# A depthwise convolution's taps on TensorE: five tiles as bands of 32 channels x 4 phases, laid out in DRAM, and a key norm one piece later

## The chip, the cores and the metric
One core of one Trainium2 chip runs the whole program. The metric is the device time of one execution, in microseconds (us); below it stands beside the span, the time from the first to the last instruction of one profiled execution.

## What is computed
A small decoder trunk on a sequence of 512 rows of 1024 channels in float32: a Conformer convolution layer, then a layer of differential attention, each followed by a gated feed-forward block. What the change touches is the first layer and one norm of the attention layer:

```python
def causal_depthwise_conv(u, w, b):           # w: 31 x 1024, one filter of 31 taps per channel
    y = lax.conv_general_dilated(u, w.reshape(width, 1, c), window_strides=(1,),
        padding=[(width - 1, 0)], dimension_numbers=('NWC', 'WIO', 'NWC'), feature_group_count=c)
    return y + b

def conformer_conv_module(x, ...):
    h = rms_norm(x, norm_g)
    u = h @ pw1_w + pw1_b
    u = u[..., :D_MODEL] * jax.nn.sigmoid(u[..., D_MODEL:])
    u = causal_depthwise_conv(u, dw_w, dw_b)
    u = jax.nn.silu(layer_norm(u, ln_g, ln_b))
    return x + u @ pw2_w + pw2_b
...
hk = rms_norm(x, kv_norm_g)                   # its mean square per row is what the "key norm" sums
k_sh = rms_norm((hk @ w_k).reshape(b, s, N_HEADS, 2, HEAD_DIM), k_norm_g)
```

## The kernel before, in words
The activations lie transposed: channels on the 128 partitions, eight tiles of 128 channels, 512 columns of sequence. Every weight matrix comes from one `stream` in units of 1 MB on SP's DMA queue into a ring of two raw slots (`w_raw`); ScalarE makes the high part of each (`split_weights`, L553), VectorE the low part (L828), and TensorE makes three float32r products for each pair (L1231). A projection unit is 48 such products.

**The convolution.** The first projection (pw1) has eight units. For each, VectorE scales the two halves (L926, L930), ScalarE takes the sigmoid (L610) and VectorE multiplies into `conv_u` (L940). Tiles 0 to 3 get their taps on VectorE: ScalarE makes the first (L623), `convolve` the other 30 (L912, L919) and the addition of two chains (L903), in pieces laid between other work. Tiles 4 to 7 get them on TensorE. ScalarE regroups each into `u2` (L619): 64 channels x 2 phases (even and odd columns) on the 128 partitions, 271 columns. A band is a matrix in which a channel's taps lie on the diagonals; TensorE makes 16 matmuls of 128x128 weights against 256 columns for it (L1304), two bands a tile, eight in all, three PSUM banks in turn (`CONV`). ScalarE copies the two phases back to `conv_c` (L630). The bands are built in DRAM by SP: `fill` writes zeros (L413), `scatter` writes single taps along the diagonals (L426), `load_band` reads rows of 2048 elements, which overlap, to 64 partitions at a time (L418), twice a band. The first two bands go into `w_raw`, the others into `band_sb`.

**The mean of the layer norm** over channels is a sum of eight matmuls with ones (L1295), laid between the bands; the last of tiles 3, 6 and 7 come after the last band. Then VectorE takes the mean away (L964, L967), and the variance follows (L1325).

**The order.** Each engine works through its own list in program order. SP's list is written out by hand: weights of units 2 and 3, the four fills, units 4 and 5, two scattered tiles, units 6 and 7, two scattered tiles, four bands, and then bands as they come free, with the first two units of pw2 among them (L451). Loads of unit n wait until unit n-2 is split.

**The key stage.** Its products are made in pieces of 12 matmuls (`dense`, L1388). After the first two, TensorE sums the squares of the residual by four small matmuls (L1397), which need GpSimd's last addition (L508); ScalarE and VectorE take the root two pieces later.

## Time and profile before

| | before |
|---|---|
| median of 3 runs | 1226.53 us (1226.29 to 1227.96) |
| the profiled execution | 1225.06 us |
| its span | 1223.3 us |
| mean granted TensorE clock | 0.993 of full |
| busy: TensorE / VectorE / ScalarE / GpSimd | 1199.7 / 788.6 / 504.6 / 61.4 us |
| DMA: packets, data | 34614, 116.77 MB |

Times of instructions are from the start of the span. "PE" is TensorE's matmul, "PEld" its weight load, which can overlap the matmul before; DVE is VectorE, ACT ScalarE, POOL GpSimd, SPq the queue on which SP issues DMAs. Matmuls are pipelined: a record's duration is longer than the distance to the next, so paces are read from starts or from totals. A float32 matmul shows as two records, a float32r one as one.

### The profile page before, as it was taken

The numbers are of one execution on the slowest core, as the hardware profiler recorded it, in microseconds if no ns is written. First come the engines' busy times: TensorE is split into PE (matmuls) and PEld (weight loads), VectorE is DVE, ScalarE is ACT, GpSimd is POOL, SyncE is SP. The second block draws the span as 40 slices with busy tenths as digits, with TensorE's granted clock in tenths as the row PEclk, the third lists the DMA queues.
The fourth block names the chain that finished last, engine by engine and source line by source line (L and its number), as shares of the span: only waits on it lengthen the run. The fifth ranks groups of instructions, "written<-read, shape, count | busy, mean of one in ns | idle before, by whom it ended". The sixth has DMA issues, their size and how long they took to land.

```text
span 1223.3 us, 16391 instructions
## 1 busy us (share of the span) xinstructions
PE 1199.7 (98%) x6106; PEld 1008.7 (82%) x6106; DVE 788.6 (64%) x1083; ACT 504.6 (41%) x814; POOL 61.4 (5%) x76
## 2 busy tenths in 40 slices
PE   8999969999999999999999999999999999999998
PEld 7888838888888888887899999987788888888887
DVE  6997945577536663676467676775677447753664
ACT  6332154543214431344656656544544224321441
POOL 1000001100000000001212021100000000000000
PEclk9999989999999999999999999999999999999999
DMA  8564802233322333223321221130232323332222
GB/s 302 137 129 113 217 19 66 73 104 103 103 72 100 103 103 103 73 82 98 103 90 39 70 70 52 56 101 7 97 102 77 131 69 103 103 103 73 99 77 95
DMA packets 34614, 116.77 MB, mean 95 GB/s; under 512 B 18304, under 2 KB 18432, under 8 KB 21888
## 3 DMA queue, kind: packets, MB, share of 16 engines
q1 hardware_dynamic: 34560, 116.03, 30.4%
q8 instruction: 36, 0.59, 0.2%
q14 instruction: 18, 0.15, 0.0%
HBM read 109.60 MB, written 6.49 MB: 95 GB/s over the span
## 4 chain that ended last, share of the span: by engine, by line
PE 92%; DVE 4%; ACT 3%; issue 1%; DMA 0%; POOL 0%; SPq 0%; POOLq 0%; DVEq 0%; ACTq 0%
PE bank L1231 71%; PE bank L1388 9%; PE bank L1304 5%; PE bank L1453 2%; PE bank L1422 1%; PE bank L1325 1%; DVE w_lo L836 1%; PE bank L1295 1%; PE bank L1270 1%; PE bank L1407 1%; ACT prob L790 0%; ACT xg_hi L570 0%; ACT w_hi L563 0%; DMA w_raw<-stream 0%; PE bank L1426 0%
## 5 line engine op out<-in xcount | busy, mean ns | idle before, releaser
L1231 PE MATMUL bank<-xg_hi,w_hi 128*128 128x512 f32 x832 | 326.7, 393 | 1.6 <-DVE xg_lo L844 1.6
L1231 PE MATMUL bank<-xg_lo,w_hi 128*128 128x512 f32 x832 | 323.8, 389 | 0.0
L1231 PE MATMUL bank<-xg_hi,w_lo 128*128 128x512 f32 x832 | 323.7, 389 | 0.0
L553 ACT ACTIVATE w_hi<-w_raw 128x2048 fp32r<-128x2048 f32 x79 | 150.7, 1907 | 149.8 <-PE bank L1231 147.1
L828 DVE TENSOR_TENSOR w_lo<-w_raw,w_hi 128x2048 fp32r<-128x2048 f32 x79 | 182.8, 2314 | 30.9 <-ACT w_hi L553 30.9
L1231 PEld LDWEIGHTS bank<-xg_hi,w_hi 128*128 128x128 f32 x832 | 156.2, 188 | 36.3 <-issue 2.2
L1231 PE MATMUL bank<-act_hi,w_hi 128*128 128x512 f32 x448 | 177.3, 396 | 7.5 <-DVE act_lo L981 7.2
L1231 PEld LDWEIGHTS bank<-xg_lo,w_hi 128*128 128x128 f32 x832 | 156.2, 188 | 33.8 <-issue 1.7
L1231 PEld LDWEIGHTS bank<-xg_hi,w_lo 128*128 128x128 f32 x832 | 156.2, 188 | 32.5
L705 ACT ACTIVATE ffn_t<-ffn_u,par 128x512 f32<-128x512 f32 x88 | 72.0, 818 | 268.7 <-DVE ffn_u L1051 268.7
L1231 PE MATMUL bank<-act_lo,w_hi 128*128 128x512 f32 x448 | 175.3, 391 | 0.0
L1231 PE MATMUL bank<-act_hi,w_lo 128*128 128x512 f32 x448 | 175.1, 391 | 0.0
L1388 PE MATMUL bank<-w_hi,xg_hi 128*128 128x256 f32 x384 | 113.5, 296 | 0.0
L1388 PE MATMUL bank<-w_hi,xg_lo 128*128 128x256 f32 x384 | 109.2, 284 | 0.0
L1388 PE MATMUL bank<-w_lo,xg_hi 128*128 128x256 f32 x384 | 109.1, 284 | 0.0
L1231 PEld LDWEIGHTS bank<-act_hi,w_hi 128*128 128x128 f32 x448 | 84.6, 189 | 27.8 <-issue 8.3
L1058 DVE SCALAR_TENSOR_TENSOR ffn_t<-ffn_u,par,ffn_t 128x512 f32<-128x512 f32 x88 | 65.9, 749 | 56.1 <-ACT ffn_t L705 56.1
L1231 PEld LDWEIGHTS bank<-act_hi,w_lo 128*128 128x128 f32 x448 | 84.7, 189 | 17.9
L1231 PEld LDWEIGHTS bank<-act_lo,w_hi 128*128 128x128 f32 x448 | 84.7, 189 | 17.3 <-issue 0.2
L996 DVE TENSOR_TENSOR x<-bank,x 128x512 f32<-128x512 f32 x48 | 33.0, 689 | 91.9 <-PE bank L1231 91.9
L1051 DVE TENSOR_TENSOR ffn_u<-bank,rs 128x512 f32<-128x512 f32 x88 | 60.6, 688 | 42.4 <-PE bank L1231 42.3
L1388 PEld LDWEIGHTS bank<-w_hi,xg_hi 128*128 128x128 f32 x384 | 74.1, 193 | 0.2 <-DVE w_lo L836 0.2
(160 smaller groups left out, 1448.8 us busy)
## 6 DMA issues: line engine op xcount, KB each, us to landing
w_raw<-stream SPq DMA_DIRECT2D x87, 1024.0 KB, 4.9
band_sb<-band SPq DMA_DIRECT2D x12, 512.0 KB, 6.9
w_raw<-stream SPq DMA_DIRECT2D x8, 768.0 KB, 4.3
band<-band_sb SPq DMA_DIRECT2D x4, 1056.0 KB, 12.3
x<-x_t SPq DMA_DIRECT2D x8, 256.0 KB, 5.8
w_raw<-band SPq DMA_DIRECT2D x4, 512.0 KB, 6.7
out_t<-x SPq DMA_DIRECT2D x8, 256.0 KB, 2.0
w_raw<-stream SPq DMA_DIRECT2D x2, 512.0 KB, 4.7
```

The costliest lines, as they stand in the source:

```text
L553: act.activation(w_hi[:, j, :], w_raw[:, j, :], ACT.Copy).then_inc(w_hi_done, 1)
L705: act.activation(ffn_t[:, 2 * j + s, :], ffn_u[:, 2 * j + s, FTAPS - 1:UP], ACT.Identity, bias=p("ffn_dw_b", at + t), scale=p("ffn_dw_w", ...
L828: dve.tensor_tensor(w_lo[:, j, :], w_raw[:, j, :], w_hi[:, j, :].bitcast(F32), sub).then_inc(w_lo_done, 1)
L836: got = dve.scalar_tensor_tensor(out=w_lo[:, j, cols], in0=w_raw[:, j, cols], scalar=p(row_gain[n], k), in1=w_hi[:, j, cols].bitcast(F32), ...
L996: new = dve.tensor_tensor(x[:, k, :], b, x[:, k, :], ALU.add)
L1051: dve.tensor_tensor(u[:, FTAPS - 1:UP], bank[2 * j + s][:, :], rs, ALU.mult).then_inc(u_done, 1)
L1058: own.wait(own.mark(dve.scalar_tensor_tensor(out=v, in0=u[:, 1:1 + SEQ], scalar=p("ffn_dw_w", w + 1), in1=v, op0=ALU.mult, op1=ALU.add)))
L1231: got = pe.matmul(out, weights(w, j, k, m), v[:, k, :], start=(k == first and s == 0), stop=(k == last and s == 2), skip_group_check=True)
L1270: pe.matmul(bank[NORM][:, :], ones[:, :], sq[:, k % 2, :], start=(k == 0), stop=(k == KT - 1), skip_group_check=True).then_inc(norm_mm if ...
L1304: got = pe.matmul(bank[CONV[n % len(CONV)]][:, 0:HALF_SEQ], band_home(n)[:, o * P:(o + 1) * P], u2[:, n, o:o + HALF_SEQ], start=o == 0, st ...
L1388: got = pe.matmul(out, v[:, k, b * P:(b + 1) * P], w[:, j, k * 2 * P:(k + 1) * 2 * P], start=(k == 0 and s == 0 and (g, at) != (0, 2)), st ...
L1453: got = pe.matmul(bank[7][:, b * VD:(b + 1) * VD], d[:, at:at + P], v[:, g % 2, k, cols], start=(k == 0 and n == 0), stop=(k == b and n == ...
```

## The change
Tile 3 moves from VectorE to TensorE, which now has five tiles. A band holds 32 channels x 4 phases: 9 matmuls against 128 columns, four bands a tile, 20 bands. ScalarE regroups a tile in 16 pieces and copies each band's output in four. SP fills five tiles with zeros before unit 3, scatters each in four transfers, copies each tile's bands inside DRAM to a new tensor `band_rows` in which a band is 128 full rows, and loads a band in one transfer. Bands 0 to 2 go to `band_sb`, 3 to 5 to `w_raw` after the projection's last split, 6 to 12 to the memory of `xg_hi` and `xg_lo` after the projection's last matmul, the others to slots that come free. VectorE sums tiles 0 to 6 into `sq_sum`; the mean is then two matmuls, one before the last band and one after the last output. In the key stage the sums of squares come after the third piece, not the second.

```diff
-DVE_TILES = [0, 1, 2, 3]
-PE_TILES = [4, 5, 6, 7]
-PHASES = 2
+DVE_TILES = [0, 1, 2]
+PE_TILES = [3, 4, 5, 6, 7]
+PHASES = 4
+CH = P // PHASES
+OFFSETS = (TAPS + PHASES - 2) // PHASES + 1
+BAND_COLS = OFFSETS * P
+BAND = (OFFSETS * PHASES + PHASES - 1) * CH
...
+RAW_BANDS = 3
+SB_BANDS = 3
+XG_BANDS = 7
...
             def load_band(n):
-                tile, h = divmod(n, 2)
+                sp.dma_start(band_home(n), band_rows[n * P:(n + 1) * P, :]).then_inc(band_in[band_slot(n)], 16)
+
+            def copy_bands(tile):
+                sp.wait_ge(band_set[tile], 16 * PHASES)
                 for r in range(PHASES):
-                    sp.dma_start(band_home(n)[r * HD:(r + 1) * HD, :],
-                                 bass.AP(band.tensor, (tile * P + h * HD) * BAND + r * HD, [[BAND, HD], [1, SLOT]])
-                                 ).then_inc(band_in[band_slot(n)], 16)
...
+                    sp.dma_start(bass.AP(band_rows.tensor, (tile * PHASES * P + r * CH) * BAND_COLS,
+                                         [[BAND_COLS, CH], [P * BAND_COLS, PHASES], [1, BAND_COLS]]),
+                                 bass.AP(band.tensor, tile * P * BAND + r * CH, [[BAND, CH], [CH * BAND, PHASES], [1, BAND_COLS]])
+                                 ).then_inc(band_copied[tile], 16)
...
+            load_unit(2)
+            for tile in range(len(PE_TILES)):
+                fill(tile)
+            load_unit(3)
+            scatter(0)
+            load_unit(4)
+            scatter(1)
+            load_unit(5)
+            scatter(2)
+            copy_bands(0)
+            scatter(3)
+            load_unit(6)
+            copy_bands(1)
+            scatter(4)
+            copy_bands(2)
+            load_unit(7)
+            copy_bands(3)
+            copy_bands(4)
+            for n in range(HOMES):
+                if n % PHASES == 0:
+                    sp.wait_ge(band_copied[n // PHASES], 16 * PHASES)
+                if n == SB_BANDS:
+                    sp.wait_ge(w_lo_done, KT)
+                if n == SB_BANDS + RAW_BANDS:
+                    sp.wait_ge(tiles, TILE0 + 2 * KT)
                 load_band(n)
...
+                if n == HOMES + SB_BANDS:
+                    for j in range(RING):
+                        sp.wait_ge(band_used, SB_BANDS + 2 + j)
+                        sp.dma_start(w_raw[:, j, :], stream[:, STARTS[KT + j]:STARTS[KT + j + 1]]).then_inc(w_in[j], 16)
...
-                    for h in range(2):
+                    for g in range(PHASES):
                         for r in range(PHASES):
-                            got = act.activation(u2[r * HD:(r + 1) * HD, n + h, :],
-                                                 conv_u[h * HD:(h + 1) * HD, m, r:CP:PHASES], ACT.Copy)
+                            at = conv_u[g * CH:(g + 1) * CH, m, r:CP:PHASES]
+                            got = act.activation(u2[r * CH:(r + 1) * CH, n + g, 0:at.shape[-1]], at, ACT.Copy)
...
-                if n in (2, 3):
+                if n in (8, 11):
                     split_weights(KT + n % 2, n % 2)
...
+            dve.wait_ge(c_done, len(DVE_TILES))
+            for n in range(KT - 2):
+                if n:
+                    dve.wait_ge(conv_summed, n)
+                if n + 1 in PE_TILES:
+                    dve.wait_ge(band_out, PHASES * (n + 2 - PE_TILES[0]))
+                if n == len(DVE_TILES) + 1:
+                    split_weights(KT + 1, 1)
+                dve.tensor_tensor(sq_sum, sq_sum if n else conv_c[:, 0, :], conv_c[:, n + 1, :], ALU.add).then_inc(conv_summed, 1)
...
-                if h == 1:
-                    if tile < len(DVE_TILES) - 1:
-                        pe.wait_ge(c_done, tile + 1)
-                        mean(DVE_TILES[tile], start=tile == 0)
-                    if tile:
-                        pe.wait_ge(band_out, 2 * tile)
-                        mean(PE_TILES[tile - 1])
-            pe.wait_ge(c_done, len(DVE_TILES))
-            mean(DVE_TILES[-1])
+                if n == BANDS - 2:
+                    pe.wait_ge(conv_summed, KT - 2)
+                    mean(sq_sum, start=True)
             pe.wait_ge(band_out, BANDS)
-            mean(PE_TILES[-1], stop=True).then_inc(mean_mm, 1)
+            mean(conv_c[:, PE_TILES[-1], :], stop=True).then_inc(mean_mm, 1)
...
-                if g == 0 and q == 1:
+                if g == 0 and q == 2:
```

## Rows read from the trace of the kernel before

**Rows 1.** The page: shares of the last chain by engine.
```profile
PE 92%; DVE 4%; ACT 3%; issue 1%; DMA 0%; POOL 0%; SPq 0%; POOLq 0%; DVEq 0%; ACTq 0%
```

**Rows 2.** The last chain in order of time: start us, us, what; 0 to 260.
```profile
23.71 74.81 PE bank L1231 x330
98.52 13.82 PE bank L1304 x64
...
158.32 2.59 PE bank L1295 x6
```

**Rows 3.** Busy time in a stretch (columns PE, PEld, DVE, ACT, POOL, clock, DMA): the convolution.
```profile
98.50:160.90 62.40, 62.40 (x275) 51.33 (x273) 47.27 (x72) 14.25 (x25) 0.00 (x0) 1.00 0.55 147
```

**Rows 4.** Timeline of VectorE (start us, us, what): the tap chains and their last additions.
```profile
106.89 0.74 DVE L919 SCALAR_TENSOR_TENSOR conv_b<-conv_u,par,conv_b 128x512 f32<-128x512 f32 x1
...
128.19 0.69 DVE L903 TENSOR_TENSOR conv_c<-conv_c,conv_b 128x512 f32<-128x512 f32 x1
```

**Rows 5.** Busy time of the warm-up matmuls (L1280) alone; columns PE, PEld, clock, DMA.
```profile
7.00:7.70 0.70, 0.70 (x8) 0.69 (x7) 1.00 0.98 383
7.60:7.70 0.10, 0.10 (x3) 0.09 (x1) 1.00 0.91 348
```

**Rows 6.** Timeline of TensorE in the attention stage.
```profile
650.78 0.27 PE L1453 MATMUL bank<-v_hi,dT_lo 128*128 128x128 f32 x1
...
653.80 0.27 PE L1453 MATMUL bank<-v_hi,dT_lo 128*128 128x128 f32 x1
...
654.20 0.28 PE L1388 MATMUL bank<-w_hi,xg_lo 128*128 128x256 f32 x1
...
655.27 0.28 PE L1388 MATMUL bank<-w_hi,xg_lo 128*128 128x256 f32 x1
```

**Rows 7.** ScalarE's copies by line (ns min/median/max), and a small one of its timeline.
```profile
L619 ACT ACTIVATE u<-conv_u x16: 433/448/462, 70.6 to 102.4; 64x271 f32<-64x271 f32 x16
L630 ACT ACTIVATE conv_c<-bank x16: 391/402/406, 105.5 to 158.8; 64x256 f32<-64x256 f32 x16
...
160.47 0.20 ACT L547 ACTIVATE small<-small 128x1 f32<-128x1 f32 x1
```

**Rows 8.** Busy time by stretch, columns as in rows 3: the clock after two waits.
```profile
163.00:168.00 5.00, 4.87 (x8) 1.93 (x8) 3.87 (x7) 2.17 (x5) 0.00 (x0) 0.66 0.00 0
592.00:598.00 6.00, 6.00 (x39) 6.00 (x40) 3.11 (x9) 5.31 (x12) 0.00 (x0) 0.72 0.00 0
```

**Rows 9.** SP's queue at the scatters: timeline, then ns of an issue, and landing.
```profile
43.41 13.43 SPq L426 DMA_DIRECT2D band<-params  x4
...
64.79 11.09 SPq L426 DMA_DIRECT2D band<-params  x4
...
L426 SPq DMA_DIRECT2D band<-params x8: 563/3070/8317, 43.4 to 71.7; - x8
DMA to landing us min/median/max: 7.4/10.9/13.8
```

**Rows 10.** Busy time by stretch, columns as in rows 3; the last is GB/s.
```profile
10.00:15.00 5.00, 3.88 (x17) 3.18 (x18) 4.96 (x8) 4.61 (x9) 0.00 (x0) 1.00 1.05 425
25.00:30.00 5.00, 5.00 (x24) 4.14 (x23) 4.96 (x4) 3.48 (x4) 0.00 (x0) 1.00 1.01 424
90.00:95.00 5.00, 5.00 (x24) 4.14 (x23) 5.00 (x9) 2.05 (x5) 0.00 (x0) 1.00 1.00 218
```

**Rows 11.** Timeline of ScalarE and VectorE: the splits of unit 7.
```profile
79.46 1.90 ACT L553 ACTIVATE w_hi<-w_raw 128x2048 fp32r<-128x2048 f32 x1
83.35 2.29 DVE L828 TENSOR_TENSOR w_lo<-w_raw,w_hi 128x2048 fp32r<-128x2048 f32 x1
```

**Rows 12.** Timeline of TensorE, VectorE and GpSimd at the sums of squares.
```profile
589.73 0.69 DVE L844 SCALAR_TENSOR_TENSOR xg_lo<-x,xg_hi 128x512 fp32r<-128x512 f32 x1 [0.70 <-ACT xg_hi L570]
590.29 1.26 POOL L508 TENSOR_TENSOR sq_sum<-sq_sum,sq 128x512 f32<-128x512 f32 x1 [0.70 <-ACT sq L573]
591.61 1.05 PE L1397 MATMUL bank<-ones,sq_sum 128*128 128x1 f32 x8 [1.99 <-POOL sq_sum L508]
```

More of the change, by code:

```diff
@@ L52 @@
 CHUNKS = [KT, KT, FT - 2 * KT]
-DVE_TILES = [0, 1, 2, 3]
-PE_TILES = [4, 5, 6, 7]
-PHASES = 2
+DVE_TILES = [0, 1, 2]
[5 more added lines that the diff above has]
+BAND = (OFFSETS * PHASES + PHASES - 1) * CH
+PHASE_SEQ = SEQ // PHASES
+PHASE_COLS = PHASE_SEQ + OFFSETS - 1
+BANDS = PHASES * len(PE_TILES)
 FIRST_PARAMS = 3 * KT
 WARM = 14
-OFFSETS = (TAPS + 1) // PHASES
-BAND = (TAPS + 2) * HD
-HALF_SEQ = SEQ // PHASES
-PHASE_COLS = HALF_SEQ + OFFSETS - 1
-BANDS = PHASES * len(PE_TILES)
+RAW_BANDS = 3
+SB_BANDS = 3
+XG_BANDS = 7
+HOMES = SB_BANDS + RAW_BANDS + XG_BANDS
+AGAIN = [n for n in range(HOMES) if not SB_BANDS <= n < SB_BANDS + RAW_BANDS]
 PARAM_WIDTHS = [
@@ L341, in trunk @@
         mean_mm = sem("mean_mm")
+        conv_summed = sem("conv_summed")
         xc_done = sem("xc_done")
@@ L389, in band_slot, with band_last @@
         def band_slot(n):
-            return n if n < 2 else 2 + n % 2
+            return n if n < HOMES else AGAIN[(n - HOMES) % len(AGAIN)]
         def band_home(n):
-            return w_raw[:, n, 0:SLOT] if n < 2 else band_sb[:, (n % 2) * SLOT:(n % 2 + 1) * SLOT]
+            at = band_slot(n)
+            if at < SB_BANDS:
+                home = band_sb
+            elif at < SB_BANDS + RAW_BANDS:
+                home, at = w_raw.rearrange("p j c -> p (j c)"), at - SB_BANDS
+            else:
+                home, at = xg_band, at - SB_BANDS - RAW_BANDS
+            return home[:, at * BAND_COLS:(at + 1) * BAND_COLS]
         def band_count(n):
-            return 32 if n < 2 else 32 * (n // 2)
+            return 16 * sum(band_slot(i) == band_slot(n) for i in range(n + 1))
+        def band_last(n):
+            return max(i for i in range(n) if band_slot(i) == band_slot(n))
         block = ctx.enter_context(nc.Block())
@@ L431, in _ @@
-            sp.wait_ge(zeros_set, 1)
-            for n in range(RING, KT, RING):
-                for j in range(RING):
-                    sp.wait_ge(w_lo_done, n + j - RING + 1)
-                    sp.dma_start(w_raw[:, j, :], stream[:, STARTS[n + j]:STARTS[n + j + 1]]).then_inc(w_in[j], 16)
-                if n == RING:
-                    for tile in range(len(PE_TILES)):
-                        fill(tile)
-                else:
-                    scatter((n - 2 * RING) // RING)
-            sp.wait_ge(band_set, 32 * len(PE_TILES))
@@ new lines, in scatter @@
+            def scatter(tile):
+                sp.wait_ge(band_zero[tile], 16)
+                for g in range(PHASES):
+                    sp.dma_start(bass.AP(band.tensor, (tile * PHASES + g) * CH * BAND + (PHASES - 1) * CH,
+                                         [[BAND + 1, CH], [CH, TAPS]]),
+                                 bass.AP(params.tensor, g * CH * N_PARAMS + PARAM_AT["dw_w"] + PE_TILES[tile] * TAPS,
+                                         [[N_PARAMS, CH], [1, TAPS]]),
+                                 allow_slow_non_contiguous=True).then_inc(band_set[tile], 16)
@@ L1291, in _, with mean @@
                     unit(2 * i + j, j, xg_hi, xg_lo, KT)
-            def mean(m, start=False, stop=False):
-                return pe.matmul(bank[NORM][:, :], ones[:, :], conv_c[:, m, :], start=start, stop=stop, skip_group_check=True)
+            def mean(v, start=False, stop=False):
+                return pe.matmul(bank[NORM][:, :], ones[:, :], v, start=start, stop=stop, skip_group_check=True)
             for n in range(BANDS):
-                tile, h = divmod(n, 2)
+                tile, g = divmod(n, PHASES)
                 pe.wait_ge(u_split, tile + 1)
@@ L1303, in _ @@
                 for o in range(OFFSETS):
-                    got = pe.matmul(bank[CONV[n % len(CONV)]][:, 0:HALF_SEQ], band_home(n)[:, o * P:(o + 1) * P],
-                                    u2[:, n, o:o + HALF_SEQ], start=o == 0, stop=o == OFFSETS - 1, skip_group_check=True)
+                    got = pe.matmul(bank[CONV[n % len(CONV)]][:, 0:PHASE_SEQ],
+                                    band_home(n)[:, o * P:(o + 1) * P], u2[:, n, o:o + PHASE_SEQ],
+                                    start=o == 0, stop=o == OFFSETS - 1, skip_group_check=True)
                 got.then_inc(band_used, 1)
-                if n == 1:
+                if n == 5:
                     pe.wait_ge(bias_summed, 1)
```

60 lines of the change are left out of this document (27 added, 33 removed).

## The prediction
> **What bounds the kernel now.** The page first: TensorE is busy for 1199.7 of 1223.3 us and carries 92% of the chain that ended last [rows 1]. So a stage gets shorter only where TensorE's own work or one of its waits gets shorter. The change lies in two places: the depthwise convolution (31 taps), and the point where the key/query stage sums its squares.
>
> The second view is the chain in order of time [rows 2]. The convolution on TensorE starts at 98.52 us and is four pieces of 13.82 us (one tile of channels, 64 records each, 216 ns a record) with the mean's matmuls between them, the last three of which, from 158.32 for 2.59 us, end at 160.91; then the layer norm begins. That makes 62.4 us, without a gap: between 98.5 and 160.9 TensorE is busy all the time at the full clock [rows 3]. So the convolution is bound by TensorE. VectorE's taps are not what ends last; its third tile ends at 128.9, waits and a weight split included [rows 4].
>
> **Part 1, the band matmuls.** Before, 8 bands x 16 offsets x 2 records (each float32 matmul shows as two) of 256 columns: 256 x 0.216 = 55.3 us for four tiles. After, 20 bands x 9 offsets x 2 = 360 records of 128 columns for five tiles. What does a record of 128 columns cost when every one has its own weight load? The warm-up matmuls have just that shape (float32, 128x128, a load each). Once the clock is up, 8 of them touch the stretch 7.00 to 7.70 and 3 touch its last 0.10 us, so five ended in 0.60 us, about 0.11 to 0.12 each [rows 5]. The attention's products with 128 columns follow each other from 650.78 to 653.80 in 27 steps, 0.112 each; 256-column float32r products, which stream about as long, go from 654.20 to 655.27 in 9 steps, 0.119 each [rows 6]. I take 0.112, the row with the same shape and the same pace: 360 x 0.112 = 40.3 us, at most 360 x 0.119 = 42.8.
>
> That rests on weight loads that run beside the matmul before them, as a load of 0.188 us (51.33 / 273) does now for every record of 0.216 us [rows 3]. The Trainium skill (TensorE: Matmul & The Clock Gate, Part 3, "What overlaps and what doesn't") says that a load overlaps matmuls in flight only when its row group differs, and all loads here use all rows. By that rule load and stream would add up; rows 5 and 6 disagree.
>
> **Part 2, the mean.** Before, eight matmuls over the tiles, 2.59 / 3 = 0.86 us each [rows 2], with a little of switching: 62.4 - 55.3 - 0.1 = 7.0 us. After, VectorE sums the first seven tiles in six additions and TensorE makes two matmuls: 0.86 and 0.1 of switching before the last band and 0.86 after the last output. The additions hide: VectorE's third tile of taps was done at 128.9 and now comes sooner (21 taps of 0.66 us remain at 106.9, so about 121) [rows 4], and the last one waits for a tile whose last band is done 3 bands (6 us) before the sum is wanted. The wait before an addition holds the split of pw2's second unit on VectorE, which nobody wants before the layer norm is over.
>
> **Part 3, ScalarE.** A tile's regrouping is now 16 pieces of 32 rows by 136, not 4 of 64 by 271 (448 ns); a band's output is 4 copies of 32x128, not 2 of 64x256 (402 ns) [rows 7]. No row has these shapes. The floor is the 0.20 us of an activation of one column [rows 7], the ceiling the old price. Half way, as length is halved: 0.32 and 0.30 us. So 16 x 0.32 = 5.2 us a tile (3.2 to 7.2) and 4 x 0.30 = 1.2 us a band (0.8 to 1.6), under the band's 2.0 us of TensorE. For tiles 3 to 6 this hides: a projection unit lasts 48 x 74.81 / 330 = 10.9 us [rows 2], and ScalarE has 0.7 + 1.9 + 5.2 us of work in it. Tile 7 does not: its regrouping starts at 101.0 (the last of four starts at 102.4) [rows 7], now ends at 106.2, and only behind it does ScalarE copy the output of band 0, done on TensorE at 100.5. The three banks are full at 104.6. Band 3 gets its bank at 106.2 + 1.2 = 107.4: **TensorE stands still for 2.8 us** (0 to 5.2). After a wait of 2.2 us the granted clock fell from 2.4 to 1.2 GHz: its mean over the next 5 us, 0.66, is 3.4 us at half; after one of 2.0 us its mean over 6 us is 0.72, again 3.4 at half [rows 8]; half of 3.4 us is lost, 1.7. At the end the last band's 1.2 us of copies stands bare before the mean's 0.86; before, two matmuls covered it.
>
> Sum of the stage: 40.3 + 0.12 (bias) + 0.96 + 2.8 + 1.7 + 1.2 + 0.86 + 0.1 = 48.0, against 62.4: **14.4 us less**. What follows (layer norm, which waits for VectorE and ScalarE) moves along unchanged.
>
> **Part 4, the DMAs.** SP fills (5 x 0.64 MB), scatters taps (20 transfers of 992 elements; before, 8 of 1984), copies each tile's bands from DRAM to DRAM (4 x 0.59 MB = 2.36 MB a tile), then loads 20 bands of 0.59 MB to all 128 partitions. Everything is on SP's one queue, past the weight loads of units 3 to 7, so each of these can be late.
> Issue: four scatters took 13.4 and 11.1 us, with 7936 elements [rows 9]; per element that is 1.55 ns, 6.2 us for a tile. A copy I give 0.6 us, the shortest issue of a scatter, which nothing held [rows 9]. Loads of units 5, 6 and 7 wait for VectorE's splits; those let 5 and 7 go just before the scatters at 43.4 and 64.8 [rows 9], and 6 half way, about 53.7. So SP does: scatter 2 till 49.9, copy 0 till 52.3, scatter 3, unit 6 at 58.8 (before: 56.9), copy 1, scatter 4 till 68, copy 2, unit 7 at 70.8 (before: 64.4), copies 3 and 4 by 76, bands 0 to 2.
> Transfer: the engines, when all busy, moved 425 GB/s in loads to 128 partitions, 424 in fills, 218 in loads to 64 [rows 10]. No transfer of before goes from DRAM to DRAM in large pieces. Bounds: 424 GB/s, if read and write overlap as in the others, 5.6 us a tile; 212, if they share that budget, 11.1. At 5.6, unit 7 lands at 80 (ScalarE wants it at 79.5, and the split for TensorE's start at 98.5 - 10.9 = 87.6 ends at 85.6, 2 us of slack [rows 11]) and band 0 at 93.5, before 98.5: nothing is lost. The new wait before each tile's copies, for scatters that landed 13.8 us after issue at most [rows 9], bites for copy 4 alone, till 82 at the latest; only the loads of bands 0 to 2 are queued behind it, and the rings are full of copies till 90 anyway. Band 0 is due in time while the five copies end by 95, (95 - 50.5 - 5 for units 6 and 7) / 5 = 7.9 us each, 298 GB/s. The mean of the bounds is 8.3, hardly late (2 us, which lie under the 2.8 us stall that ScalarE makes anyway). I take **no loss**, and as the other end 11.1: copies end at 111, band 0 lands at 114.5, 16 us late; less the 2.8 us stall it replaces, that costs 13.2.
> Later loads are covered: bands 6 to 12 start at 98.5, 1.4 us each against 2.0 us of use; pw2's first weights leave at about 112 and are wanted at 121.
> The Trainium skill (DMA: Bandwidth & Descriptors, "Latency and other measured facts") gives 207 GB/s per direction for DMA copies of tiles between HBM tensors. If that means one direct copy, it speaks against this change: by that page's figure, as an estimate, a tile's copies take 11.4 us and the kernel 1223.7. No row of before decides it.
>
> **Part 5, the key stage.** TensorE stood 1.99 us before the sums of squares, waiting for GpSimd's last addition (590.29 + 1.26), and the clock fell to half for 3.4 us after it [rows 8, 12]. One more piece (12 records of 0.119 = 1.43 us) now runs first; its operand was there at 590.4 [rows 12]. The sums finish when they did, so ScalarE's chain keeps its time: 1.43 us gained, and with an idle of 0.56 us the clock should hold, 1.7 more. **3.1 us** (1.4 to 3.1).
>
> **How the numbers follow.** 14.4 + 3.1 = 17.5 us. The profiled execution took 1225.06 (span 1223.3, 1.8 around it), so 1207.6; it lies 1.5 under the median of 1226.53, and carried over to the median that is **1209.0**.
>
> Rivals:
> 1. **Copies late, but not past the gain** (8 to 11.1 us a tile, or issue behind): each us over 7.9 costs up to 5, from 1209.0 to 1209.0 + 13.2 = 1222.2. Half rate is a natural limit for a copy that both reads and writes the same memory; against it, the fills show that writing alone is no slower than reading. Chance 0.24.
> 2. **Copies that become the bound: slower.** From 1222.2 another 4.3 us must go to reach 1226.5, 0.9 us a tile, so from 12.0 us a tile (197 GB/s) on the change loses. At 15 us a tile (157 GB/s) it is 1222.2 + 5 x 3.9 = 1242, and unit 7 lands so late that TensorE also stops within the projection. For it: nothing shows a copy's rate, and scatters of 4-byte pieces stand between the copies. Against it: every large transfer of before ran at 218 GB/s or more. Chance 0.11.
> 3. **A scatter costs per transfer, not per element.** Issues took 3.07 us in the median [rows 9]; if 992 elements take as long as 1984, a tile's scatter is 12.3 us, SP is behind by some 14 us at unit 6 and 20 at unit 7, and the bands come 20 to 25 us late: 1209 + 22 = 1231, slower. Against it: one issue took 0.56, another 8.3 us. Chance 0.06.
> 4. **Loads don't overlap at 128 columns**: 360 x (0.112 + 0.108, half a record of 256) = 79.2 instead of 40.3, 1248. Rows 5 and 6 speak against it, and the Trainium skill's rule named above for it. Chance 0.01.
> 5. **The change does less than it says**: ScalarE's copies (over 0.5 us each, outside my bounds) or VectorE pace the stage; 20 x 2.4 = 48 instead of 40.3 gives 1217. Chance 0.06.
>
> The forecast itself has 0.52. Its own range is 1204.5 (no stall and no clock loss, 4.5 less) to 1214 (2.5 for 0.119 a record, 2.4 more stall). The range of 8 in 10 goes on up through rival 1: 1204.5 to 1224, which leaves rivals 2 to 4 out, 0.18. A measurement here tells about 0.2%, 2.5 us, from no change. Faster by more than that: 0.52 + 0.21 of rival 1 + 0.06 = 0.79. Within it: 0.03 of rival 1 and 0.03 of rival 2. Slower: 0.08 + 0.06 + 0.01 = 0.15.
>
> **What would show it.** Steps of 0.112 us between the band records; one idle of about 3 us before band 3, put down to ScalarE, with a lower clock behind it; no TensorE wait for a band or for unit 6 or 7; DRAM-to-DRAM copies at over 300 GB/s; layer norm starting at about 146.5; TensorE's wait for GpSimd at 0.6 us. I am wrong if the first band lands after 100 us, if ScalarE is busy without a gap after 107, or if the projection's last unit starts later than 87.6.

## The result, and the profile after

The change makes the kernel slower by 0.4%: 1230.95 us (median of 13 runs, 1228.87 to 1233.68) against 1226.53 (13 runs), ratio 1.0038 [1.0030, 1.0047]. The forecast was 1209.0, with a range up to 1224. The profiled execution took 1230.69 us, span 1228.9, mean clock 0.985. Below, L1284 are the projections' products (L1231 before), L1357 the bands, L1348 the mean; L452 is a scatter, L444 a copy within DRAM, L461 the load of a weight unit, L439 that of a band; L666 is ScalarE's regrouping, L676 its copy of a band's output.

First the shares of the last chain; in [rows 1] SPq and DMA had 0%.

```profile
PE 84%; DVE 7%; ACT 5%; SPq 2%; DMA 1%; issue 1%; POOL 0%; DVEq 0%; ACTq 0%
```

Second, TensorE's waits between 20 and 170 us (engine, line, releaser: us in total, times, longest). Before, the same stretch had no wait for `w_lo` and none for ScalarE's copies of outputs (`conv_c`); the 2.2 us for `ln_sq` stood there too.

```profile
PE bank L1284 <- DVE w_lo L874: 13.4, 2, 10.8
PE bank L1357 <- ACT conv_c L676: 5.8, 2, 5.6
PE bank L1373 <- ACT ln_sq L688: 2.2, 1, 2.2
PE bank L1348 <- ACT conv_c L676: 1.7, 1, 1.7
```

Third, the chain in order of time (start us, us, what). It leads from SP's issues to the load of unit 7, its two splits, the projection's last unit and the bands.

```profile
66.31 3.78 SPq L444
...
72.38 4.48 SPq L452
76.91 4.15 SPq L452
...
86.04 11.77 DMA w_raw<-stream
97.83 1.92 ACT w_hi L599
99.77 2.30 DVE w_lo L874
102.12 13.27 PE bank L1284 x48
...
126.96 7.93 PE bank L1357 x54
...
167.40 0.76 DVE conv_a L1017
```

The last unit takes 13.1 us from its start to that of the first band, and not 10.9, because the clock is low after its wait. The columns of the next view are those of [rows 3]; behind the 10.8 us wait for `w_lo` and the 5.6 us one for ScalarE the granted clock is at or near its lower level.

```profile
102.00:108.00 6.00, 5.88 (x17) 4.65 (x18) 5.43 (x10) 5.54 (x12) 0.00 (x0) 0.62 1.02 336
...
124.00:128.00 4.00, 1.04 (x5) 1.07 (x6) 4.00 (x7) 3.87 (x10) 0.00 (x0) 0.50 1.02 421
```

**The account.** The bands start at 115.22, not at 98.52 as in [rows 2]: 16.7 us late. The two waits are 2.65 and 10.78 us, the clock behind the second costs 115.22 - 102.12 - 10.9 = 2.2, 0.7 was there before unit 6, and 0.3 are the ends of the records before the two waits, which otherwise lie under the next record. The stage from there to the layer norm takes 167.40 - 115.22 = 52.2 us, against 62.4 before and 48.0 in the forecast. So the layer norm starts 6.5 us late instead of 14.4 early. Its variance matmuls take 10.1 us instead of 9.2 (the clock again: from 169 to 180 us its mean is 0.74, where before it is 0.84 over the same 11 us, 163 to 174), and the key stage gives some 3 us back: 6.5 + 0.9 - 3.1 = 4.3, against 4.4 between the medians. The change did shorten the stage, by 10.2 us; the projection ahead of it got longer by more.

**SP's queue** is where the forecast and the trace part. Its timeline (start us, us, line, issues):

```profile
43.75 0.33 SPq L461 DMA_DIRECT2D w_raw<-stream  x1
44.13 5.30 SPq L452 DMA_DIRECT2D band<-params  x4
49.47 6.21 SPq L444 DMA_DIRECT2D band_rows<-band  x4
55.73 8.39 SPq L452 DMA_DIRECT2D band<-params  x4
64.16 1.53 SPq L461 DMA_DIRECT2D w_raw<-stream  x1
65.73 5.92 SPq L444 DMA_DIRECT2D band_rows<-band  x4
71.69 10.08 SPq L452 DMA_DIRECT2D band<-params  x4
81.81 4.18 SPq L444 DMA_DIRECT2D band_rows<-band  x4
86.04 0.65 SPq L461 DMA_DIRECT2D w_raw<-stream  x1
```

Scatter 2 ends at 49.4, forecast 49.9: still right. From the first copy on everything stretches. Four copies take 4 to 6 us instead of 2.4, a scatter behind copies 8.4 and 10.1 instead of 6.2. Unit 6 leaves at 64.2 (forecast 58.8), unit 7 at 86.0 (forecast 70.8, before 64.4). Of these 15 us about 9 are the issues of three tiles' copies (6.21 + 5.92 + 4.18 against 7.2) and about 6 those of two tiles' scatters (8.39 + 10.08 against 12.4).

The 16 DMA engines aren't full meanwhile: from 65 to 85 us the mean of their shares is 0.67, at 176 GB/s (columns as in [rows 3]; whether a single one is full it doesn't tell).

```profile
65.00:85.00 20.00, 17.35 (x77) 14.02 (x76) 15.57 (x23) 12.63 (x26) 0.00 (x0) 1.00 0.67 176
```

### The profile page after: what moved, and what is told of

Read it like the earlier page. It is cut to its first block, busy times and chain, and to the rows that moved or that the text cites. A ratio compares the mean times of both kernels' runs of the same rounds, so it can differ in the third digit from the quotient of the medians.

```text
span 1228.9 us, 16730 instructions
## 1 busy us (share of the span) xinstructions
PE 1185.7 (96%) x6198; PEld 1002.1 (82%) x6198; DVE 772.8 (63%) x1059; ACT 557.6 (45%) x941; POOL 60.7 (5%) x76
## 4 chain that ended last, share of the span: by engine, by line
PE 84%; DVE 7%; ACT 5%; SPq 2%; DMA 1%; issue 1%; POOL 0%; DVEq 0%; ACTq 0%
PE bank L1284 66%; PE bank L1436 9%; PE bank L1501 2%; PE bank L1357 2%; DMA w_raw<-stream 1%; PE bank L1470 1%; DVE w_lo L874 1%; ACT conv_c L676 1%; PE bank L1373 1%; DVE conv_c L966 1%; SPq L452 1%; SPq L444 1%; ACT w_hi L599 1%; DVE w_lo L882 1%; DVE conv_b L966 1%
## 5 line engine op out<-in xcount | busy, mean ns | idle before, releaser
L1284 PE MATMUL bank<-xg_hi,w_hi 128*128 128x512 f32 x832 | 327.9, 394 | 15.5 <-DVE w_lo L874 13.4
L1284 PE MATMUL bank<-xg_lo,w_hi 128*128 128x512 f32 x832 | 324.5, 390 | 0.0
L1284 PE MATMUL bank<-xg_hi,w_lo 128*128 128x512 f32 x832 | 324.5, 390 | 0.0
L1284 PEld LDWEIGHTS bank<-xg_hi,w_hi 128*128 128x128 f32 x832 | 156.7, 188 | 51.1 <-DVE w_lo L874 14.3
L1284 PE MATMUL bank<-act_hi,w_hi 128*128 128x512 f32 x448 | 177.3, 396 | 7.5 <-DVE act_lo L1034 7.2
L1284 PEld LDWEIGHTS bank<-xg_lo,w_hi 128*128 128x128 f32 x832 | 156.8, 188 | 33.7 <-issue 1.7
L1284 PEld LDWEIGHTS bank<-xg_hi,w_lo 128*128 128x128 f32 x832 | 156.6, 188 | 32.7
L1284 PE MATMUL bank<-act_lo,w_hi 128*128 128x512 f32 x448 | 175.4, 391 | 0.0
L1284 PE MATMUL bank<-act_hi,w_lo 128*128 128x512 f32 x448 | 175.2, 391 | 0.0
L1284 PEld LDWEIGHTS bank<-act_hi,w_hi 128*128 128x128 f32 x448 | 84.7, 189 | 27.9 <-issue 8.3
L1111 DVE SCALAR_TENSOR_TENSOR ffn_t<-ffn_u,par,ffn_t 128x512 f32<-128x512 f32 x88 | 65.9, 749 | 56.1 <-ACT ffn_t L751 56.1
L1284 PEld LDWEIGHTS bank<-act_hi,w_lo 128*128 128x128 f32 x448 | 84.7, 189 | 18.0
L1284 PEld LDWEIGHTS bank<-act_lo,w_hi 128*128 128x128 f32 x448 | 84.7, 189 | 17.2 <-issue 0.2
L1114 DVE SCALAR_TENSOR_TENSOR ffn_t<-ffn_u,par,ffn_t 128x512 f32<-128x512 f32 x88 | 66.2, 752 | 12.5 <-DVE ffn_t L1111 12.2
## 6 DMA issues: line engine op xcount, KB each, us to landing
band_rows<-band SPq DMA_DIRECT2D x20, 576.0 KB, 10.2
band<-band_sb SPq DMA_DIRECT2D x5, 624.0 KB, 10.8
```

What stands on the lines that cost most here:

```text
L1111: own.wait(own.mark(dve.scalar_tensor_tensor(out=v, in0=u[:, 1:1 + SEQ], scalar=p("ffn_dw_w", w + 1), in1=v, op0=ALU.mult, op1=ALU.add)))
L1114: dve.scalar_tensor_tensor(out=v, in0=u[:, 0:SEQ], scalar=p("ffn_dw_w", w), in1=v, op0=ALU.mult, op1=ALU.add).then_inc(taps_done, 1)
L1284: got = pe.matmul(out, weights(w, j, k, m), v[:, k, :], start=(k == first and s == 0), stop=(k == last and s == 2), skip_group_check=True)
```

## The experiments

Each ratio is against runs of the kernel before on the same chip (its medians were 1225.7 to 1226.8). "Before" and "after" are the two kernels of the change.

| kernel | us | ratio [95%] |
|---|---|---|
| norm_only | 1223.31 | 0.9973 [0.9960, 0.9985] |
| units_first | 1221.88 | 0.9967 [0.9952, 0.9983] |
| no_build | 1214.59 | 0.9905 [0.9890, 0.9921] |
| no_copies | 1214.57 | 0.9903 [0.9888, 0.9918] |
| no_scatter | 1215.22 | 0.9909 [0.9886, 0.9933] |
| rows_scatter | 1214.33 | 0.9904 [0.9888, 0.9921] |
| copies_on_gpsimd | 1227.97 | 1.0015 [1.0000, 1.0031] |
| late_split | 1214.74 | 0.9907 [0.9888, 0.9925] |
| dve_regroup | 1216.24 | 0.9920 [0.9892, 0.9948] |
| contiguous_regroup | 1211.38 | one run |
| no_build_dve_regroup | 1208.39 | 0.9855 [0.9838, 0.9873] |
| fitted_order | 1215.10 | 0.9907 [0.9893, 0.9921] |
| dense_scatters | 1212.77 | 0.9898 [0.9883, 0.9912] |
| spaced_scatters | 1213.84 | 0.9910 [0.9892, 0.9929] |

### The key norm alone

One condition of the kernel before:

```diff
-                if g == 0 and q == 1:
+                if g == 0 and q == 2:
```

> The kernel before with the key norm's sums one piece later and nothing else. Theory A (the prediction's part 5): 1.43 us of TensorE's wait goes and the clock does not fall after it, 3.1 us less in all: 1223.4. Rival: the wait is shorter but later waits of the attention give part of it back, 1.5 us less: 1225.0. TensorE's wait for GpSimd falls from 1.99 to 0.55 us either way.

1226.36 - 1223.31 = 3.05 us, as forecast (3.1); the interval of the ratio makes it 1.8 to 4.9 us, which leaves the rival's 1.5 out. The wait before the sums is 0.52 us. In after it is 0.54, where [rows 12] had 1.99, and the clock behind it 1.00, where [rows 8] had 0.72 (TensorE's timeline, then a stretch):

```profile
599.12 1.05 PE L1445 MATMUL bank<-ones,sq_sum 128*128 128x1 f32 x8 [0.54 <-POOL sq_sum L554]
```
```profile
600.50:606.50 6.00, 6.00 (x53) 6.00 (x52) 3.09 (x9) 4.31 (x9) 0.00 (x0) 1.00 0.00 0
```

### Is it SP's order? The weight units first

```diff
             scatter(2)
-            copy_bands(0)
             scatter(3)
             load_unit(6)
-            copy_bands(1)
             scatter(4)
-            copy_bands(2)
             load_unit(7)
-            copy_bands(3)
-            copy_bands(4)
+            copy_bands(0)
+            copy_bands(1)
             for n in range(HOMES):
+                if n == SB_BANDS:
+                    copy_bands(2)
+                if n == SB_BANDS + RAW_BANDS:
+                    copy_bands(3)
+                    copy_bands(4)
```

> The changed kernel with SP's list in another order: all scatters and the weights of units 6 and 7 before the first copy; the copies follow, each before the bands that need it. Theory A (the changed kernel loses its gain because SP's queue delivers the weights of units 6 and 7 late: waits of 2.65 and 10.78 us, and 2.4 us in unit 7 at the low clock): the projection ends near 99 instead of 115.2, the kernel takes 1231 - 15.8 = 1215. Rival B (the copies take so much transfer time that the bands are late instead): TensorE waits for bands by 10 us or more, 1225 or above.

1221.88: 9 us faster than after, and no wait for `w_lo` any more. But TensorE now waits 10.5 us for ScalarE, 5.5 of them before band 3, the rest because ScalarE waits for pw2's first weights (issued at 119.8, landed at about 135) and holds back the bands' outputs meanwhile. The order was a cause; another wait took part of its place.

### Which part of the band building holds SP?

Three kernels leave out parts of it; their bands do not hold the taps. `no_build`: no fills, scatters or copies, the bands are read from `stream`. `no_copies`: fills and scatters stay. `no_scatter`: fills and copies stay.

The first diff is that of no_build and no_copies, beside the calls that they leave out; the second that of no_scatter.

```diff
             def load_band(n):
-                sp.dma_start(band_home(n), band_rows[n * P:(n + 1) * P, :]).then_inc(band_in[band_slot(n)], 16)
+                sp.dma_start(band_home(n), stream[:, n * BAND_COLS:(n + 1) * BAND_COLS]).then_inc(band_in[band_slot(n)], 16)
```
```diff
             def copy_bands(tile):
-                sp.wait_ge(band_set[tile], 16 * PHASES)
+                sp.wait_ge(band_zero[tile], 16)
```

> The changed kernel without fills, scatters and copies; the 20 bands are read as rows of the weight stream, so the taps are wrong numbers, all else is done. It gives the price of building the bands. Theory A: with the weights on time the projection ends near 98.5 and nothing else of the building is on the path: 1215, the same as with the weights' loads first. Rival: bands themselves are also late in the changed kernel, or the traffic slows other stages: then this kernel is faster than the reordered one by over 3 us.

> The changed kernel without the copies inside DRAM only (bands read as rows of the weight stream, wrong taps); fills and scatters stay in their places. Theory A1 (copies hold SP's queue: 6.2 + 5.9 + 4.2 us of issue before unit 7, and their data stand ahead of it): unit 7 issues at about 70, lands at 75, TensorE does not wait, 1215. Rival A2 (the scatters are what holds the queue, 8.4 and 10.1 us for tiles 3 and 4, whatever stands beside them): unit 7 still issues at 80 or later and TensorE still waits 5 us or more, 1221 to 1226.

> The changed kernel without scatters (the copies move zeros, so the taps are missing); fills and copies stay in their places. If SP is held by whatever the engines still have to do, each copy of a tile holds it about 7 us (2.36 MB at 340 GB/s) beyond a small start: unit 6 issues at 54, unit 7 at 70 or before, lands by 78; no wait of TensorE. If the copies alone are enough to delay unit 7, it issues after 75 and TensorE waits 3 us or more.

1214.6, 1214.6 and 1215.2 (two runs): the scatters alone cost nothing that these runs tell, nor do the copies alone. Only both together cost 16.4 us (1230.95 - 1214.59). SP's timeline of no_copies, where two tiles' scatters take 11.03 us:

```profile
43.94 11.03 SPq L452 DMA_DIRECT2D band<-params  x8
55.01 1.82 SPq L461 DMA_DIRECT2D w_raw<-stream  x1
56.88 7.32 SPq L452 DMA_DIRECT2D band<-params  x4
64.93 0.40 SPq L461 DMA_DIRECT2D w_raw<-stream  x1
```

and of no_scatter, where four copies take 2.6 us:

```profile
44.02 2.63 SPq L444 DMA_DIRECT2D band_rows<-band  x4
54.34 0.33 SPq L461 DMA_DIRECT2D w_raw<-stream  x1
54.72 5.24 SPq L444 DMA_DIRECT2D band_rows<-band  x8
65.03 0.33 SPq L461 DMA_DIRECT2D w_raw<-stream  x1
```

Either way unit 7 leaves at 65. So the numbers with which the prediction summed SP's time (1.55 ns per element, 0.6 us per copy) hold roughly for each kind alone, and fail for the two mixed. Busy engines don't hold SP like this by themselves: in no_scatter their share is 0.90 from 45 to 65 us and 1.01 from 65 to 85, at 345 and 350 GB/s, and a tile's copies still take 2.6 us of issue, not the 7 that they would if SP waited for their data.

### The number of transfers, or that of pieces?

In rows_scatter the taps lie in the wrong places of the bands, and the pieces are 32 runs of 31 elements for each transfer.

```diff
                     sp.dma_start(bass.AP(band.tensor, (tile * PHASES + g) * CH * BAND + (PHASES - 1) * CH,
-                                         [[BAND + 1, CH], [CH, TAPS]]),
+                                         [[BAND + 1, CH], [1, TAPS]]),
```

> The changed kernel, except that each scatter transfer writes its 992 taps as 32 runs of 31 neighbouring elements instead of 992 single elements along the diagonals; the bands so hold the taps in the wrong places, all sizes, waits and SP's order are as they were. Theory A (the price of scatters beside copies is that of their many 4-byte pieces, which fill the queue): issues of a tile's scatter fall to about 2 to 3 us, unit 7 is issued near 65 as in no_scatter, no wait for a weight unit, about 1215 us. Rival B (it is a price per transfer, or the waits between scatters and copies, whatever the pieces): SP's timeline stays as in the changed kernel, unit 7 issued at 86, 1228 to 1231 us.

1214.33. Sizes, waits, number of transfers and order are those of after; only the 992 single elements are 32 runs. SP:

```profile
44.34 2.39 SPq L452 DMA_DIRECT2D band<-params  x4
46.78 2.53 SPq L444 DMA_DIRECT2D band_rows<-band  x4
49.35 2.83 SPq L452 DMA_DIRECT2D band<-params  x4
...
65.34 0.33 SPq L461 DMA_DIRECT2D w_raw<-stream  x1
```

A scatter behind copies now takes 2.8 us, not 8.4. The copies' issues shrink too, from 6.2 us to 2.5. What holds SP is thousands of small pieces (3968 a tile) beside large transfers. That also refutes rival 3 of the prediction (a price per transfer), though its 1231 us came true.

### Does another queue help?

`copy_bands` moves from SP's list to GpSimd's.

```diff
             pool.memset(zeros, 0.0).then_inc(zeros_set, 1)
...
+            for tile in range(len(PE_TILES)):
+                copy_bands(tile)
```

> The changed kernel with the copies inside DRAM issued by GpSimd, which is idle then; all else in its order. Theory A (it is the order within one queue that delays the weights, not what the engines can move): units 6 and 7 issue at 55 and 65, no wait of TensorE for them, 1215 to 1217. Rival B (the 16 engines are simply full): the weights of unit 7 still land after 85 and TensorE waits 3 us or more, 1220 and up.

1227.97, only 3 us faster than after, and no faster than before. SP issues no copy, and its scatters are held more than ever (its L444 is the scatter here, L453 the unit's load):

```profile
45.98 19.15 SPq L444 DMA_DIRECT2D band<-params  x8
65.18 5.28 SPq L453 DMA_DIRECT2D w_raw<-stream  x1
70.50 17.98 SPq L444 DMA_DIRECT2D band<-params  x4
88.53 0.66 SPq L453 DMA_DIRECT2D w_raw<-stream  x1
```

GpSimd's four copies take 2.1 to 2.4 us each time. TensorE waits 8.4 us for `w_lo`. The time is the one that rival B gave, but the engines aren't simply full either: their share is 0.71 from 45 to 65 us and 0.81 from 65 to 85. So the wait is not one of order within SP's queue alone. A reading that fits the four runs is that the scatters' issue goes on only as their pieces go through the engines, and that these give turns to 4.6 KB pieces of copies in between. It is not shown: no run here looks into the queue.

### The order mended

`late_split` is units_first with pw2's weights issued right behind band 12, ScalarE's splits of them after bands 12 and 15 (8 and 11 before), and VectorE's behind its additions.

```diff
-                if n in (8, 11):
+                if n in (12, 15):
                     split_weights(KT + n % 2, n % 2)
...
-            split_weights(KT, 0)
...
-                if n == len(DVE_TILES) + 1:
-                    split_weights(KT + 1, 1)
...
+            split_weights(KT, 0)
+            split_weights(KT + 1, 1)
```

> The reordered kernel (scatters and weights of units 6 and 7 before the copies) with one more thing moved: the weights of pw2's first two units go out right behind band 12 and not behind band 15, ScalarE splits them after bands 12 and 15 and not 8 and 11, VectorE splits them after its additions. Theory A: the reordered kernel lost its last part because ScalarE, waiting 5.7 us for those weights, held back band outputs and so TensorE (10.5 us of waits for ScalarE against 5.8); without it 1215. Rival: with the copies in the same queue something else is late, 1219 or more.

1214.74: the kernel with all its work is as fast as without building the bands (1214.59), and 12 us faster than before. The stall before band 3 stays, 5.5 us.

### ScalarE's regrouping

In no_build the last tile's 16 copies take 7.32 us (timeline of ScalarE):

```profile
102.59 7.32 ACT L650 ACTIVATE u<-conv_u 32x136 f32<-32x136 f32 x16 [0.99 <-DVE conv_u L971]
```

`contiguous_regroup` is no_build with neighbouring columns read instead of every fourth (wrong values, same shapes); `no_build_dve_regroup` is no_build with those 16 copies on VectorE.

The diff is that of contiguous_regroup.

```diff
-                            at = conv_u[g * CH:(g + 1) * CH, m, r:CP:PHASES]
+                            at = conv_u[g * CH:(g + 1) * CH, m, 0:(CP - r + PHASES - 1) // PHASES]
```

> The kernel without band building (as in no_build), except that ScalarE's regrouping reads 135 or 136 neighbouring columns instead of every fourth one, so that u holds wrong values; shapes, writes and waits are the same. Theory A (a 32x136 copy costs as much as a 64x271 one because it reads every fourth column, over the same span of memory): the copies fall from 0.455 to about 0.32 us each, and the stall before band 3 from 5.5 to about 3.5 us. Rival B (the price is one of the instruction, not of its stride): 0.45 us each again, stall 5.5 us. The time would be 1212.5 by A and 1214.6 by B.

> The kernel without band building (as in no_build), and the last tile's 16 regrouping copies on VectorE (4.6 us) instead of ScalarE. Theory A (of the 5.6 us by which the stage without late weights is still longer than forecast, ScalarE's regrouping of tile 7 is the cause): the stall before band 3 is gone or under 1 us, the clock stays at its high level, about 1207 to 1209 us. Rival B (VectorE's regrouping delays the third tile's taps, and their sum, or the copies of outputs pace the stage): 1212 or more, with a wait for VectorE or ScalarE elsewhere in the band phase.

```profile
102.00 5.20 ACT L650 ACTIVATE u<-conv_u 32x136 f32<-32x136 f32 x16 [0.99 <-DVE conv_u L971]
```

5.20 us, 0.325 each, which is what the prediction took for the strided copies; the stall before band 3 is 3.4 us. So most of the surplus is the price of the stride. 136 elements at a step of four cost what 271 at a step of two cost [rows 7], and the step of two seems to cost nothing: from 136 neighbours (0.32 us) to 271 elements at a step of two (0.45) it is 0.9 to 1.0 ns for each further element. The time, 1211.38 in one run, is 3.2 us under no_build. 2.1 us are the stall; in the two profiled executions the variance matmuls also take 0.7 us less (9.29, 9.99) and the bands start 0.6 sooner, while the 54 records behind the stall are no shorter (7.89, 7.75).

VectorE makes the same 16 copies in 4.6 us (0.29 each), and 1208.39 is what the change with this one move would bring if the bands came for nothing. That it lies at the forecast's 1209.0 is luck: this kernel has no stall for ScalarE and no low clock behind one, for which the forecast had 4.5 us.

### All of it together, three orders

`dve_regroup` is late_split with the last tile's regrouping on VectorE. `fitted_order` also splits pw2's units after bands 10 and 13 and puts copy 3 before bands 6 to 11 and copy 4 before band 12. `dense_scatters` is fitted_order with the scatters packed into SP's idle time, so that copies start sooner, and `spaced_scatters` moves scatter 4 behind unit 6.

The first diff is dve_regroup's, the second fitted_order's, the third SP's list from after to dense_scatters; spaced_scatters puts scatter(4) behind unit 6, and copy_bands(1) behind unit 7.

```diff
+                if m == KT - 1:
+                    dve.wait_ge(c_u, KT)
...
+                    for g in range(PHASES):
+                        for r in range(PHASES):
+                            at = conv_u[g * CH:(g + 1) * CH, m, r:CP:PHASES]
+                            got = dve.tensor_copy(u2[r * CH:(r + 1) * CH, n + g, 0:at.shape[-1]], at)
```
```diff
                 if n == SB_BANDS + RAW_BANDS:
                     copy_bands(3)
-                    copy_bands(4)
+                if n == HOMES - 1:
+                    copy_bands(4)
...
-                if n in (12, 15):
+                if n in (10, 13):
```
```diff
             load_unit(4)
             scatter(1)
-            load_unit(5)
             scatter(2)
-            copy_bands(0)
+            load_unit(5)
             scatter(3)
+            scatter(4)
             load_unit(6)
+            copy_bands(0)
             copy_bands(1)
-            scatter(4)
-            copy_bands(2)
             load_unit(7)
-            copy_bands(3)
-            copy_bands(4)
+            copy_bands(2)
             for n in range(HOMES):
+                if n == SB_BANDS:
+                    copy_bands(3)
+                if n == SB_BANDS + RAW_BANDS:
+                    copy_bands(4)
```

> The same, and VectorE makes the 16 regrouping copies of the last tile, not ScalarE. Theory A: TensorE's wait of 5.5 us before band 3 goes and the clock does not fall behind it (about 2): 1215 - 7.5 = 1207.5. Rival: VectorE's taps and additions end later and become what the mean waits for, or the clock falls anyway: 1210 or more.

> The changed kernel with all its work, in an order fitted to SP's queue: all scatters and units 6 and 7 ahead of every copy; copies 0 and 1, bands 0 to 2, copy 2, bands 3 to 5, copy 3, bands 6 to 11, copy 4, bands 12 and on; pw2's weights behind band 12, split on ScalarE after bands 10 and 13 and on VectorE after its additions; the last tile's regrouping on VectorE. Theory A (what was lost was the order on the queue and ScalarE's regrouping, nothing of the work itself): no wait for a weight unit, no idle over 1 us in the band phase, 1207 to 1210 us, as without building the bands. Rival B (the engines are too full of copies between 66 and 110 us whatever the order, and a band load lands late somewhere): an idle of 2 us or more before band 0, 3, 6 or 12 that nothing but the queue explains, 1213 to 1217 us.

> The changed kernel with all its work and the last tile's regrouping on VectorE, as in fitted_order, but SP uses its idle time between the weight units: scatters 1 and 2 between units 4 and 5, scatters 3 and 4 between 5 and 6, then copies 0 and 1, unit 7, copy 2, bands 0 to 2, copy 3, bands 3 to 5, copy 4, bands 6 on. The copies so start at 55 to 57 us instead of 67. Theory A (what fitted_order still loses, 6.8 us of TensorE waits before bands 6, 13 and 14, is a backlog of the DMA engines, which are full from 67 to 135 us because the scatters let no copy start before): copies end about 10 us sooner, no wait for a weight unit or a band over 1 us, 1207 to 1210 us, the time without any building (1208.4). Rival B (copies and band loads together are too much for the engines wherever they start, or scatters packed one behind the other stop SP, so that unit 6 or 7 is late): waits of 3 us or more stay, or a weight unit is waited for, 1213 us or more.

> dense_scatters, except that only scatter 3 stands between units 5 and 6, and scatter 4 and copy 0 between units 6 and 7 (copies 1 and 2 behind unit 7). In dense_scatters scatters 3 and 4 together held unit 6 to 61.9 and TensorE waited 3.0 us in the projection. Theory A (SP's issue timeline is all that is left): units 6 and 7 issued by 56 and 66, no wait for weights, no wait for a band over 1 us, 1208 to 1210 us. Rival B (the copies' bytes, with a band phase that starts 5 us sooner, are late again): no wait for weights, but 2 to 5 us of waits before bands 6 to 16 that only the queue explains, 1211 to 1214 us.

1216.24, 1215.10, 1212.77, 1213.84: none reaches 1208.4. In dve_regroup the stall for ScalarE is gone, but TensorE stands 4.2 us before band 6, whose load landed at 116.53, 17 us after its issue and 0.1 before TensorE went on. In fitted_order it is three waits, before bands 6, 12 and 13 (not 6, 13 and 14, as the expectation of dense_scatters counts). They are "issue" in the profile because no engine had to finish anything; the loads of bands 12 and 13 landed at 126.91 and 133.22 (two lines of TensorE's timeline, then the DMA share and GB/s at the end of two stretches):

```profile
127.00 2.25 PE L1370 MATMUL bank<-u,xg_band 128*128 128x128 f32 x18 [1.96 <-issue]
133.31 7.80 PE L1370 MATMUL bank<-u,band_sb 128*128 128x128 f32 x54 [4.07 <-issue]
```
```profile
67.00:100.00 33.00, 33.00 (x152) 27.51 (x152) 30.50 (x44) 27.87 (x56) 0.00 (x0) 1.00 1.00 342
100.00:135.00 35.00, 27.62 (x235) 27.05 (x234) 29.30 (x59) 22.93 (x54) 0.00 (x0) 0.97 1.02 412
```

The engines are full from 67 to 135 us and move 33 x 0.342 + 35 x 0.412 = 25.7 MB. no_build moves 33 x 0.138 + 35 x 0.315 = 15.6 MB in the same time; the rest is the copies (11.8 MB in all), less loads that now end behind 135 us. dense_scatters has no wait for a band over 0.3 us, but two tiles' scatters before unit 6 took 15.3 us, and TensorE waits 3.0 us for `w_lo`; its bands also start 5 us later than in the others, at 103.8, which gives their loads time. spaced_scatters has no wait for weights, and one of 3.5 us before band 6:

```profile
115.65 15.94 PE L1369 MATMUL bank<-u,xg_band 128*128 128x128 f32 x126 [3.55 <-issue]
```

dve_regroup reached the time of its rival (1210 or more), but by a wait that the rival didn't name. fitted_order and spaced_scatters came out as their rival B said, dense_scatters by its second half (a weight unit is late). Some 4 to 8 us remain, which three orders only move about. late_split does not show them because its 5.5 us stall for ScalarE lies over the late loads: band 6 landed at 117.0, and TensorE came to it at 120.2. Whether the rest is the price of the copies' bytes or of an order that was not tried stays open. For the bytes speaks that band 6 landed between 112.7 and 117.0 us in late_split and in all four kernels of this section, whatever the order, and TensorE is ready for it at about 112 when nothing before it is late. dense_scatters has the lowest time with all the work, 0.9898 of before and 18 us less than after, but its interval overlaps those of late_split, fitted_order and spaced_scatters.

## Why the prediction was wrong, step by step

- **Part 1, band matmuls: right.** In after 54 records go from 115.22 in 6.03 us, 0.112 each; nowhere a load that adds to its matmul. In the Trainium skill (TensorE: Matmul & The Clock Gate, Part 3, "What overlaps and what doesn't") the rule on row groups would have made it twice that; the trace speaks against it here.
- **Part 2, the mean: right in kind.** Two matmuls, no wait for VectorE's sums; the last took 1.14 us instead of 0.86. That isn't the clock, which is 1.00 from 166 to 168 us: 0.86 is the distance from one such matmul to the next, and the last one has no other behind it, so that its full duration counts.
- **Part 3, ScalarE: mechanism right, size wrong.** The stall came where it was forecast, before band 3, put down to ScalarE, at 5.55 us instead of 2.8. The mis-sized terms are "half way, as length is halved: 0.32 and 0.30 us": a regrouping copy took 0.45 us, a band's copy 0.40, the ceilings. The clock behind it cost 1.7, as forecast: 54 records from 126.96 in 7.76 us, not 6.03. Of the stage's 4.2 us too much, 2.75 are the stall and 0.46 the last output's copies (1.66 for 1.2); 0.28 are the last mean matmul.
- **Part 4, transfer: right.** Copies ran at 386 GB/s where hardly anything else ran (late_split, 72 to 79 us), and with band loads among them at 346 (80 to 90), above the 298 from which the sum lost nothing. The figure of 207 GB/s of the Trainium skill (DMA: Bandwidth & Descriptors, "Latency and other measured facts") is not what direct copies give here; that page's row is for pieces of 16 KiB at a row pitch of 512 KiB, these copies have pieces of 4.6 KB at a pitch of 5.0 KB, and no run here tries the page's form.
- **Part 4, issue: this step failed.** "So SP does: ... unit 6 at 58.8 ..., unit 7 at 70.8" adds issues as if each had its own price (6.2 us for a tile's scatter, 0.6 for a copy), whatever else is under way. Scatters and copies mixed took 8.4 and 10.1 us for a tile's scatter and 1.0 to 1.6 for a copy. Unit 7 left 15 us later than that, and with its landing (11.8 us after issue, forecast 9) TensorE stood 10.8 us within the projection, which the sum did not hold at all. Without this term after would be at 1214.6 (no_build), 5.6 over the forecast, of which ScalarE's part is 3.2 and the longer variance matmuls 0.8 (9.99 for 9.2). Two of the prediction's signs of being wrong came: the first band landed at 113.3 ("after 100"), and the projection's last unit started at 102.1 ("later than 87.6"). The warning was in [rows 9]: one form of issue took from 0.56 to 8.3 us. I used the mean for a price and the spread only to refute a rival; such a spread says that an issue can wait for something.
- **Part 4, the later loads: not seen.** Forecast as covered, they were in after, but only because everything before them was late: with the projection on time, the copies and band loads fill the engines to 135 us, and band 6's load landed 17 us after its issue (dve_regroup). pw2's first weights, forecast to leave at 112, left at 119.8 and landed at 135.3 in units_first, which cost TensorE 5 us.
- **Part 5, key norm: right**, 3.05 us for 3.1.
- **The rivals.** Rival 1 named "issue behind" but capped it at 1222.2, since it let only the bands be late and not unit 7. Rival 3 put SP 20 us behind at unit 7 (measured 15) and 14 at unit 6 (measured 5), and gave 1231, from a cause that rows_scatter refutes; that its number came true is luck. It had 0.06. Rival 2 had the stop within the projection, but by a slow copy, not by a queue.

## What to carry to other kernels

Before transfers of many small pieces are put on a queue, ask what stands behind them and is due: their issue can hold the queue, and here it held it longest while large copies ran, from the same queue or another. Put loads with a due time ahead of them, and large DRAM copies behind both. When one stall is removed, look for what it lay over: here a 5.5 us stall for ScalarE covered band loads that were as late.

## What the runs showed of the hardware

- A transfer of 992 single elements issued in 1.3 to 1.9 us in the mean of a tile where no copy ran (5.30 / 4 in after, 15.33 / 8 in dense_scatters), but in 2.3 beside fills (scatter 0 of after, 9.13 / 4) and also in scatter 4 of spaced_scatters (9.27 / 4), with no copy under way. Behind copies it was 2.1 to 2.5 us (8.39 / 4, 10.08 / 4); the longest took 12.5 us, beside copies from another queue. As 32 runs it took 0.6 to 0.7 behind copies.
- A copy's own issue took 0.6 to 0.7 us without such scatters (2.63 / 4 in no_scatter), and 1.0 to 1.6 among them (4.18 / 4 to 6.21 / 4 in after), with the engines 0.67 busy.
- ScalarE's copy of 32 rows by 136 columns took 0.325 us from neighbours and 0.45 at a step of four; 271 columns at a step of two took 0.45 as well [rows 7]. VectorE took 0.29 for 136 at a step of four.
- A copy within DRAM in pieces of 4.6 KB reached 386 GB/s, close to a load's 425 [rows 10].
